# Later small loads and constants, rows normed by three engines, and another order of the first transposes, in a one-core decoder layer with experts

## The reference

```python
def _modulation(c, w_mod, b_mod):
    m = jax.nn.silu(c) @ w_mod + b_mod
    return jnp.split(m[:, None, :], 6, axis=-1)

def _trunk_layer(x, c, ...):
    sh1, sc1, gt1, sh2, sc2, gt2 = _modulation(c, w_mod, b_mod)
    h = _rmsnorm(x, g_pre_mix) * (1.0 + sc1) + sh1
    aq, af, ai, ag, bq, bk, bv, gate_a, gate_b = jnp.split(h @ w_in, IN_SPLITS, axis=-1)
    o_a, s_new = _hgrn2(aq, af, ai, ag, s_hgrn0, lb, g_hgrn)      # linear recurrence, 4 heads
    o_b = ...                                                     # differential attention, 4 heads
    merged = jax.nn.sigmoid(gate_a) * (o_a @ w_proj_a) + jax.nn.sigmoid(gate_b) * (o_b @ w_proj_b)
    x = x + gt1 * _rmsnorm(merged @ w_out, g_post_mix)
    h2 = _rmsnorm(x, g_pre_ffn) * (1.0 + sc2) + sh2
    x = x + gt2 * _rmsnorm(_moe(h2, ...), g_post_ffn)             # top 4 of 32 experts
```

## Time and profile before

| | us |
|---|---|
| median of 3 runs | 1284.89 |
| lowest, highest | 1284.45, 1287.19 |
| the profiled execution, as timed | 1288.25 |
| its span, first to last instruction | 1286.5 |

### The profile page before, as it was taken

The page is one execution under the profiler, slowest core; times in us unless marked ns, Lnnn a source line. Parts: engine busy times, 40 slices in busy tenths (PEclk is TensorE's granted clock), DMA queues, the critical chain, the costliest instruction groups (busy, mean ns, idle before and its releaser), DMA issues.

```text
span 1286.5 us, 23726 instructions
## 1 busy us (share of the span) xinstructions
PE 1095.7 (85%) x9780; PEld 466.4 (36%) x9780; DVE 600.4 (47%) x1129; ACT 224.4 (17%) x371; POOL 59.6 (5%) x106
## 2 busy tenths in 40 slices
PE   6899999999979687897696997999966996667996
PEld 3576676776433122231131322333311331112332
DVE  2246843433665434363352563656622552233654
ACT  3001420040411111111010210112100110110112
POOL 2102011120020000000000000000000000000000
PEclk9899999999979989998898998999978998788998
DMA  9879894677799999999999999899999999999996
GB/s 338 268 258 340 282 324 150 191 265 278 283 394 426 427 429 428 428 428 427 428 428 428 427 429 428 370 425 428 428 427 429 428 427 427 428 428 427 429 428 251
DMA packets 67282, 486.16 MB, mean 378 GB/s; under 512 B 6013, under 2 KB 28882, under 8 KB 40426
## 3 DMA queue, kind: packets, MB, share of 16 engines
q1 hardware_dynamic: 59584, 462.11, 87.1%
q0 software_dynamic: 6496, 19.48, 4.6%
q10 hardware_dynamic: 1130, 3.50, 0.7%
HBM read 479.31 MB, written 5.77 MB: 377 GB/s over the span
## 4 chain that ended last, share of the span: by engine, by line
DMA 44%; PE 26%; DVE 1%; issue 0%; ACT 0%; DVEq 0%; ACTq 0%
DMA big<-in_w_down 27%; PE PB L1128 13%; DMA big<-in_w_gate_up 11%; PE PB L1155 7%; DMA hTG<-in_w_down 5%; PE PB L1089 2%; PE PB L1097 1%; PE PB L1113 1%; PE PB L1104 1%; PE PB L1121 0%; PE PB L1074 0%; DVE big L1452 0%; DVE cst L1449 0%; DVE big L1449 0%; ACT L1395 0%
## 5 line engine op out<-in xcount | busy, mean ns | idle before, releaser
L1128 PE MATMUL PB<-big,cst 128*32 128x512 f32 x2768 | 353.6, 654 | 108.8 <-DMA big<-in_w_gate_up 108.8
L2032 DVE TENSOR_TENSOR tok<-PB,cst 32x512 f32<-32x512 f32 x188 | 129.2, 687 | 258.8 <-ACT cst L1394 256.9
L1128 PEld LDWEIGHTS PB<-big,cst 128*32 128x32 f32 x2768 | 88.6, 115 | 345.1 <-issue 182.3
L1155 PE MATMUL PB<-big,cst 128*32 128x512 f32 x1408 | 165.0, 597 | 24.2 <-DMA big<-in_w_down 24.2
L716 PE MATMUL PB<-hTG,big 128*128 128x264 f32 x576 | 139.3, 396 | 2.2 <-DVE hTG L1446 1.5
L2009 DVE TENSOR_SCALAR mod<-PB 64x512 f32<-64x512 f32 x48 | 33.3, 693 | 206.4 <-PE PB L1128 206.4
L716 PEld LDWEIGHTS PB<-hTG,big 128*128 128x128 f32 x576 | 108.9, 194 | 31.4 <-issue 14.1
L1389 ACT ACTIVATE mod<-PB 64x512 f32<-64x512 f32 x48 | 28.4, 591 | 417.8 <-PE PB L1128 417.8
L1089 PE MATMUL PB<-wide,att 128*32 128x256 f32 x1176 | 79.1, 402 | 6.6 <-DVE att L2004 6.6
L1155 PEld LDWEIGHTS PB<-big,cst 128*32 128x32 f32 x1408 | 39.0, 109 | 107.5 <-issue 64.9
L1389 ACT ACT_TABLE_LOAD x48 | 61.6, 1283 | 1.8 <-ACT small L1382 0.9
(11 more groups left out here) (336 smaller groups left out, 924.6 us busy)
## 6 DMA issues: line engine op xcount, KB each, us to landing
big<-in_w_gate_up SPq DMA_DIRECT2D x115, 2048.0 KB, 30.8
big<-in_w_down SPq DMA_DIRECT2D x57, 2048.0 KB, 24.4
hTG<-in_w_gate_up SPq DMA_DIRECT2D x13, 2048.0 KB, 38.1
big<-in_w_mod SPq DMA_DIRECT2D x24, 1024.0 KB, 8.4
big<-in_w_in SPq DMA_DIRECT2D x22, 1024.0 KB, 8.0
hTG<-in_w_down SPq DMA_DIRECT2D x6, 2048.0 KB, 24.0
wide<-in_cache_k POOLq DMA_DIRECT2D x16, 256.0 KB, 5.7
hTG<-in_cache_v POOLq DMA_DIRECT2D x16, 256.0 KB, 3.4
```

The costliest lines, as they stand in the source:

```text
L1128: mm = pe.matmul(GU[32 * j:32 * j + 32, :], mo["xT"][:, (2 * u + r) * M:(2 * u + r + 1) * M], groups(w[:, r * 2 * D:(r + 1) * 2 * D])[:, j ...
L1155: mm = pe.matmul(DN[32 * j:32 * j + 32, :], mo["actT"][:, (4 * u + r) * M:(4 * u + r + 1) * M], w[:, r * D + half * 512:r * D + (half + 1) ...
L2032: mm = dve.tensor_tensor(mo["y"][rows, :], DN[rows, :], mo["y_part"][other, :], ALU.add)
```

## The change

Five edits:

- Pool's small loads wait for hT_ready at 16, the shifted hT.
- The rest of the constants is asked for when ACT has taken bq3.
- The rows are squared and normed by three parties: ACT squares chunks 0 and 2 and DVE chunk 1 (a product and a reduction); DVE multiplies chunks 0 and 1 and ACT chunk 2. xn_ready is raised three times. ACT does a root of a constant ahead of the squares.
- TensorE's order sc0, sc1, sc2, four x_T, sc3, four x_T becomes sc0, sc1, four x_T, sc2, four x_T, sc3.
- ACT's exponential for the forget gate's bound (lbe_ready) comes behind the eight evictions of hT.

```diff
--- before.py
+++ after.py
@@ -492,7 +492,7 @@
                            bass.AP(a["b_mod"].tensor, 0, [[256, 4], [D, 2], [1, 256]])).then_inc(S("bmod_loaded"), 16)
             pool.memset(mod[:, 1:3, :], 0.0).then_inc(S("zeroed"), 1)
 
-            pool.wait_ge(S("hT_ready"), KC)
+            pool.wait_ge(S("hT_ready"), 2 * KC)
             pool.wait_ge(S("zeroed"), 1)
             for j in range(4):
                 src = bass.AP(a["b_mod"].tensor, 2048 + j * 512, [[0, 9], [2048, 2], [1, 512]])
@@ -748,7 +748,7 @@
             def x_T(k):
 
                 bank = begin(f"xt{k}")
-                pe.wait_ge(S("xn_ready"), 1)
+                pe.wait_ge(S("xn_ready"), 3)
                 for c in range(NCH):
                     n = rows_of[c]
                     mm = tr(bank[:, c * P:c * P + n], xn[0:n, c, k * P:(k + 1) * P], n)
@@ -934,13 +934,14 @@
                     mm = pe.matmul(bank[0:NS, E:2 * E], SH2[:, k, 1:9], wr[:, k, :], start=(k == 0), stop=(k == KC - 1))
                 full(mm)
 
-            for i in range(3):
-                scale_part(i)
+            scale_part(0)
+            scale_part(1)
             for k in range(4):
                 x_T(k)
-            scale_part(3)
+            scale_part(2)
             for k in range(4, KC):
                 x_T(k)
+            scale_part(3)
             first_cols("mt0", 1)
             in_T(FIRST, [], [(shift_part, 0), (shift_part, 1)], [(shift_part, 2), (shift_part, 3)], [(first_unit_shift,)])
             in_T(5, [(first_unit_cols,)], [], [], [])
@@ -1223,20 +1224,24 @@
             act.wait_ge(S("vt_ready"), 1)
             do(act.activation(VTs[:, 0:72], VT[:, 0:72], ACT.Sigmoid), "csig_ready")
 
+            act.wait_ge(S("ssq_zero"), 1)
+            do(act.activation(sv("sl"), eps[:, :], ACT.Sqrt))
             act.wait_ge(S("x_loaded"), 32)
-            act.wait_ge(S("ssq_zero"), 1)
-            for c in range(NCH):
+            for c in (0, 2):
                 n = rows_of[c]
                 do(act.activation(hTf[0:n, 0:D], x[0:n, c, :], ACT.Square,
                                   accum_out=sv("ssq", c, c + 1, n)))
+            act.wait_ge(S("ssq_zero"), 2)
             do(act.activation(sv("rs"), sv("ssq"), ACT.Sqrt, scale=1.0 / D, bias=eps[:, :]), "rms_ready")
-            act.wait_ge(S("vt_ready"), 2)
-            do(act.activation(sv("lb", 4, 12), sv("lb", 4, 12), ACT.Exp), "lbe_ready")
+            act.wait_ge(S("xn_ready"), 1)
+            do(act.activation(xn[0:NS, 2, :], x[0:NS, 2, :], ACT.Copy, scale=sv("rs", 2, 3, NS)), "xn_ready")
             for k in range(KC):
                 act.wait_ge(S("aux_full"), AUX[f"xt{k}"] + 1)
                 act.wait_ge(S("aux_free"), AUX[f"xt{k}"])
                 do(act.activation(hT[:, k, :], aux(f"xt{k}")[:, 0:T], ACT.Copy))
                 act.nop().then_inc(S("aux_free"), 1)
+            act.wait_ge(S("vt_ready"), 2)
+            do(act.activation(sv("lb", 4, 12), sv("lb", 4, 12), ACT.Exp), "lbe_ready")
 
             def bank(name):
                 i = PROJ[name]
@@ -1265,7 +1270,7 @@
 
             for j in range(H):
                 take(QT, "bq", j, scale=0.125)
-                if j == 0:
+                if j == H - 1:
                     act.dma_start(cst[:, P + E:], a["consts"][:, P + E:]).then_inc(S("cst_loaded"), 16)
             act.wait_ge(S("lam_dots"), 1)
             do(act.activation(sv("lam", 2, 4), sv("lam", 0, 2), ACT.Exp), "lam_exp")
@@ -1472,11 +1477,13 @@
             dve.wait_ge(S("csig_ready"), 1)
             do(dve.tensor_tensor(cT[:, :, 0:9], VT[:, 0:72].rearrange("p (r k) -> p k r", r=9),
                                  VTs[:, 0:72].rearrange("p (r k) -> p k r", r=9), ALU.mult), "cT_ready")
+            dve.wait_ge(S("x_loaded"), 32)
+            tt(hTf[:, D:2 * D], x[:, 1, :], x[:, 1, :], ALU.mult)
+            do(dve.tensor_reduce(sv("ssq", 1, 2), hTf[:, D:2 * D], AX, ALU.add), "ssq_zero")
             dve.wait_ge(S("rms_ready"), 1)
-            do(dve.reciprocal(sv("rs"), sv("rs")))
-            for c in range(NCH):
-                n = rows_of[c]
-                ts(xn[0:n, c, :], x[0:n, c, :], sv("rs", c, c + 1, n), None, ALU.mult)
+            do(dve.reciprocal(sv("rs"), sv("rs")), "xn_ready")
+            for c in range(2):
+                ts(xn[:, c, :], x[:, c, :], sv("rs", c, c + 1), None, ALU.mult)
             dve.nop().then_inc(S("xn_ready"), 1)
             def mod_rows(g):
                 dve.wait_ge(S("mod_used"), 4 + KC * g)
```

## The result

The changed kernel takes 1293.77 us, the median of 13 runs (1286.76 to 1300.18); the kernel before, beside it, 1286.26 (1282.38 to 1293.56, 13 runs). The ratio is 1.0044 [1.0025, 1.0063], which is some 5.7 us (the medians themselves lie 7.5 apart): slower, where 8.5 us of gain were forecast. Four runs of the changed kernel lie at 1286.8 to 1287.6 and nine at 1292.7 to 1300.2, with nothing between. The kernel before has no such gap.

The account below looks back on a forecast made before the run. The expert-weight DMA stream was taken as the bound, its start set by the routing table and TensorE's early wait for shift pieces. 8.82 - 0.1 - 0.2 = 8.5 us off median 1284.89 gave 1276.4, range 1273.8 to 1281.5.

Parts of the forecast that it names:

- The reading of the stream: Expert weights, 376 to 1242 us: they stream without a break, so a microsecond won ahead of the routing table shortens the end.
- The wait goes, unit 5 is earlier: TensorE after bq2: no wait for the last shift pieces (5.93), faster matmuls behind it (1.71 and 1.18), 8.82 us in sum.
- Taking this for the kernel: Whole kernel: the 8.5 us gain, read from one profiled execution, was taken from the three-run median 1284.89, giving 1276.4.
- The units of the stream: w_in halves for TensorE's next unit: delayed by the constants asked for ahead of them; loss 0.2 us, bounds 0 and 5.
- The half microsecond of cover: Unit 5's second half of w_in: asked for at 45.6, landing after 8.5, wanted at 54.6, so just in time.
- The 36% free: DMA engines from 60 to 80 us: busy at 0.64, so the loads were taken to have slack there.
- Rival 1: Between 44 and 62 us: the displaced loads collide, one or two waits of 1 to 3 us; 1278 to 1281.5; chance 0.20.
- Rival 4: DVE before the queries' copy: expert biases land late and hold TensorE's fourth transposing step; slower, 1290 with latency 25; chance 0.06.
- The front at -0.1: Norming by three engines and the new transpose order at the start: a loss of 0.1 us, bounds gain 0.6, loss 1.8.
- The bound named for a slow pace: First four transposes at the start: if they run at the pace of scale piece 1, a loss of 1.8 us.
- Rival 3: Between 100 and 366 us: something not moving with TensorE takes the gain back; 1282 to 1285; chance 0.07.

## Why the prediction was wrong

Predicted was 1276.4 in 1273.8 to 1281.5, with a chance of 0.06 for slower; it came out slower.

1. *The reading of the stream: right.* The span less the table's end is 920.9 in the earlier trace rows's execution and 919.6 to 921.5 in all the other profiles, whose tables come between 355.3 and 378.1. What is won ahead of the table is won at the end.
2. *The wait goes, unit 5 is earlier: right for that execution.* 5.93 + 1.71 + 1.18 were there; unit 5 came 7.4 earlier, with 1.7 lost to a lower granted clock in unit 4 (0.50 from 26 to 28 us). TensorE had stood 1.48 for hT ahead of it, but in the kernel before it stood 1.49 there and took 7.36, and two other kernels with the new front (gains late, constants behind the keys) took 7.36 as well; so the edits are not what lowers it, and what does is open. The fourth piece landed at 20.4 + 15.1 = 35.5; forecast was 36.
3. *Taking this for the kernel: the first step that failed.* The gain was read from one execution and subtracted from the median. In executions with a late front the wait of 5.93 does not exist. An estimate from the counts: 6 early of 15, times 8.8, is 3.5 us; the variants whose profiles show neither wait got 2.1 to 4.2 (0.9984 to 0.9967). The 3.4 us between the profiled run and the median of three were in view; they were treated as scatter and not as a sign that executions differ in what they wait for. None of the rivals was this one.
4. *"The units of the stream", priced at 0.2, bounds 0 and 5: mis-sized.* It measured 9.0 (6.2 of wait, 2.8 of lower clock) in the early execution and 9.3 (6.5 + 2.7) in the late one. The half microsecond of cover was looked for at unit 5's second half and held there: asked for at 46.88, landed 8.9 later, forecast 8.5. For this term the queue was not followed one unit further, where the next half of w_in stands behind a w_mod piece and meets nearly all of Pool's loads. The estimate went by MB and the 400 GB/s of the earlier trace rows; in the stage of the collision full engines moved 227. The 36% free of the earlier trace rows are read from 60 to 80 us; the stretch that was to become 44 to 62 (53 to 71 of the kernel before) was at 0.65, so that reading did no harm.
5. *Rival 1* (0.20) was the right mechanism, and its sign, a wait for w_in at 54 or 62 us, came at 64.3. Its price was too low: it left a gain of 3.5 to 7 us, so the collision was to cost 1.5 to 5, and it cost 9.0. It was argued from the turns of the packets. The Trainium skill, DMA: Bandwidth & Descriptors, section "Queues, rings and completion order", says that an engine goes round its queues packet by packet; here 508 packets of Pool's passed beside 732 of SP's, less than turn by turn over the whole (from 57 to 60 us it was 210 beside 54), and yet took the larger share of the engines, 0.598 x 144 us / 508 = 170 ns a packet against 86. Turns alone do not price a collision; the time of each packet does.
6. *Rival 4* did not happen. The copy of the sample queries came at 77.59, later than the 76 that was named as its sign, but DVE waited for TensorE there, not for the biases. Its ingredient was seen, though: lambda landed at about 61, the worst time that the prediction worked out, and DVE waited 7.5 us for it at no cost.
7. *The front at -0.1: right within what can be told.* 0.9996 [0.9982, 1.0009] alone; unit 4 started at 23.88 (24.2 was forecast). The bound named for a slow pace (a loss of 1.8) also showed: in the late execution of the changed kernel both groups of four transposes took 3.35, and unit 4 began at 28.51, where the kernel before with a late front has 27.03.
8. *Rival 3* stays small: from unit 6's start to the table the profiles scatter between 290 and 297 us, with no wait that belongs to the change, and two at 301 and 303, of which one holds the 4.4 named above.

Put together, as an estimate: in early executions 8.8 won and 9.0 lost, in late ones nothing won and some 10 lost; with nine of thirteen runs late that is about 7 us, and 0.44% is 5.7. It takes the nine runs of the upper group for the late ones, and the kernel before for late as often.

What stays open is why the front is early or late. The pace of TensorE between 14 and 26 us differs (16 matmuls in 1.07 or 1.94 us), though the granted clock reads 1.00 there in both kinds. The Trainium skill, TensorE: Matmul & The Clock Gate, section "Seeing it yourself", warns that clock events in traces of trn2 have been seen to be unreliable; the rows here agree, since one reading stands beside two paces. That six matmuls ahead of it went with an early front in three profiles of three speaks for the clock, and doesn't prove it: with 6 early of 15, three in a row come by chance about once in 16 times.

## What to carry to other kernels

A wait that is read from one execution must be looked for in a second before its price is subtracted from a median: what releases a competing load may move with the engine's own pace, and the collision comes and goes with it. When loads are put later, follow every transfer that is queued beside them until they have all landed, and price them by the time their packets hold the engines, not by their bytes. Two kinds of place did well here, and can't be told apart: tied to the landing of what must go first (0.9977, 0.9984), or behind the point where the ring has slack (0.9973). And two moves that are each harmless alone may not go to the same place.

## What the runs showed of the hardware

- Two queues of small rows together fell to 227 GB/s at a share of the engines near 1, in a stretch where one queue alone, with some large rows in it, moved 268 GB/s at 0.74. A transfer of 1 MB in 1 KB rows took 15.3 us in place of 5.2.
- A front that is 3 us slower made a transfer land 7 us sooner (23.2 against 16.4), with what competed with it held back as well (Pool's loads by 2.9 us, the constants by 4.3).
- TensorE did 16 equal matmuls in 1.07 or in 1.94 us in the same place, by execution, at a granted clock of 1.00 in both.
- The granted clock between 200 and 340 us was lower by sums of 0 to 6.8 us (the length times one less the clock) from execution to execution, in steps of about 1.7, and TensorE had no wait above 1.8 us in that stretch in any of them: some 3 us of scatter on either side, as large as what most of these edits are worth.
